# The opening of a two-block kernel: norm sums on GpSimd, one load queue, matmuls on zeros, and a gate unit in two passes

## The reference

```python
def rmsnorm(x, g):
    xf = x.astype(jnp.float32)
    y = xf * lax.rsqrt(jnp.mean(xf * xf, axis=-1, keepdims=True) + EPS)
    return (y * g.astype(jnp.float32)).astype(x.dtype)

h = rmsnorm(x, ln_g[l])
proj = h @ w_in[l]            # split into g_u, g_v, ..., d_a, d_b, c_q, c_z
g = -jnp.exp(dn_a_log) * jax.nn.softplus(d_a + dn_dt_bias)
beta = jax.nn.sigmoid(d_b)
m = rmsnorm(mem, mem_norm_g[l])
mk, mv = jnp.split(m @ w_mem_kv[l], 2, axis=-1)
```

## Time and profile before

| | us |
|---|---|
| median of 3 runs | 2020.8 (2020.19 to 2021.98) |
| the profiled execution | 2021.16 |
| its span | 2019.6 |
| PE busy | 1981.8 (98%) |
| DVE busy | 1135.0 (56%) |
| ACT busy | 838.9 (42%) |
| POOL busy | 144.1 (7%) |

### The profile page before, as it was taken

One profiled execution on the slowest core, in us unless ns is written; L12 is line 12 of the kernel. 1 busy time (PEld: TensorE's weight loads), 2 busy tenths in 40 slices (PEclk: granted clock), 3 DMA queues, 4 the chain that ended last, 5 costly groups with the idle time before them and its releaser, 6 DMA issues.

```text
span 2019.6 us, 28731 instructions
## 1 busy us (share of the span) xinstructions
PE 1981.8 (98%) x9560; PEld 1647.7 (82%) x9560; DVE 1135.0 (56%) x1982; ACT 838.9 (42%) x1627; POOL 144.1 (7%) x174
## 2 busy tenths in 40 slices
PE   7999999999999999999999999999999999998999
PEld 6788788888888888788878888888888888887887
DVE  5643576777767775643355454545454545455332
ACT  5543444444444443533245353535353535354211
POOL 1100011121111210011000000000000000000110
PEclk9999999999999999999999999999999999998999
DMA  9522231222322212244422222222222222222441
GB/s 364 197 95 83 73 94 64 72 73 73 75 76 77 73 63 76 81 159 149 150 99 84 89 83 88 83 88 83 88 83 88 83 88 83 88 83 86 153 151 68
DMA packets 33394, 202.32 MB, mean 100 GB/s; under 512 B 4528, under 2 KB 4656, under 8 KB 12624
## 3 DMA queue, kind: packets, MB, share of 16 engines
q1 hardware_dynamic: 23040, 164.64, 22.8%
q0 software_dynamic: 10176, 37.13, 6.4%
q10 hardware_dynamic: 144, 0.10, 0.0%
HBM read 193.43 MB, written 8.42 MB: 100 GB/s over the span
## 4 chain that ended last, share of the span: by engine, by line
PE 93%; ACT 2%; DVE 2%; DMA 1%; issue 1%; POOL 0%; DVEq 0%; ACTq 0%; SPq 0%; POOLq 0%
PE gemm L1222 80%; PE pb L1222 12%; PE pb L1225 2%; DMA scratch<-in_memT 1%; ACT scratch L613 0%; DMA raw<-in_w 0%; ACT w_hi_t L617 0%; ACT scratch L615 0%; ACT scratch L368 0%; DVE scratch L1094 0%; DMA scratch<-in_rows_in 0%; DVE w_lo_t L1138 0%; DVE w_lo L663 0%; ACT w_hi L327 0%; DVE scratch L1133 0%
## 5 line engine op out<-in xcount | busy, mean ns | idle before, releaser
L1222 PE MATMUL gemm<-act_lo,w_hi 128*128 128x512 f32 x2512 | 979.2, 392 | 12.2 <-DVE act_lo L684 10.2
L1222 PE MATMUL gemm<-act_hi,w_hi 128*128 128x512 f32 x2384 | 956.7, 401 | 13.2 <-DVE act_lo L672 10.5
L1222 PE MATMUL gemm<-act_hi,w_lo 128*128 128x512 f32 x2384 | 932.5, 391 | 0.0
L1222 PEld LDWEIGHTS gemm<-act_lo,w_hi 128*128 128x128 f32 x2512 | 475.9, 189 | 106.3 <-issue 14.5
L1222 PEld LDWEIGHTS gemm<-act_hi,w_hi 128*128 128x128 f32 x2384 | 449.7, 189 | 105.3 <-issue 19.3
L1222 PEld LDWEIGHTS gemm<-act_hi,w_lo 128*128 128x128 f32 x2384 | 448.5, 188 | 96.3
L327 ACT ACTIVATE w_hi<-raw 128x512 fp32r<-128x512 f32 x624 | 341.0, 618 | 407.7 <-PE gemm L1222 394.8
L663 DVE TENSOR_TENSOR w_lo<-raw,w_hi 128x512 fp32r<-128x512 f32 x624 | 402.6, 701 | 189.8 <-ACT w_hi L327 188.0
L1222 PEld LDWEIGHTS pb<-scratch 128*128 128x128 f32 (+1 forms) x1248 | 163.3, 188 | 29.2 <-DVE scratch L989 4.9
L1222 PE MATMUL pb<-scratch 128*128 128x64 f32 (+4 forms) x1248 | 173.4, 277 | 1.5 <-DVE scratch L989 1.2
L265 POOL TENSOR_TENSOR scratch<-scratch,cst 128x512 f32<-128x512 f32 x56 | 78.4, 1405 | 433.7 <-DVE scratch L882 262.4
(11 more groups left out here) (226 smaller groups left out, 1453.8 us busy)
## 6 DMA issues: line engine op xcount, KB each, us to landing
raw<-in_w SPq DMA_DIRECT2D x156, 1024.0 KB, 4.8
scratch<-in_rows_in POOLq DMA_DIRECT2D x6, 1024.0 KB, 6.1
big<-in_xT POOLq DMA_DIRECT2D x4, 1024.0 KB, 11.8
scratch<-rows POOLq DMA_DIRECT2D x16, 256.0 KB, 6.0
scratch<-in_xT POOLq DMA_DIRECT2D x16, 256.0 KB, 3.0
x<-big POOLq DMA_DIRECT2D x16, 256.0 KB, 2.3
scratch<-x POOLq DMA_DIRECT2D x16, 256.0 KB, 4.0
outT<-scratch POOLq DMA_DIRECT2D x16, 256.0 KB, 3.8
```

Source lines behind the costliest of these rows:

```text
L1222: return nc.tensor.matmul(out, a, b, start=start, stop=stop, skip_group_check=skip)
```

## The change

It does five things.

- The norm sums no longer come from row-major copies. ACT squares the feature-major tiles (memT in place, xT into free tiles), POOL adds the squares up with nine additions (`fold` and three additions of 128 x 2048), and PE multiplies the remaining tile with ones. ACT takes the root on the spread result. `rows_in`, the diagonals and their loads are gone.
- memT and xT are loaded by SP's queue, between the weights: w quarter, memT quarter, four times; then the quarters of w 1; then w 2, xT 0, w 3, xT 1 and so on. POOL loads only the constants, after unit 1 has been multiplied.
- PE begins with six fp32 matmuls on a tile of zeros.
- The gate unit holds high and low part of its 64 used columns side by side in one stationary operand, and needs two matmuls a k step, not three; the two halves are added after the transposes.
- The sums over ones come after step 3 of unit 9; the gate transposes come before the ones of the memory values, and both factors of the memory projection are applied before these transposes.

Shortened to what matters:

```diff
-MT, XT = 2, 4
-ROW_AT = {3: 0, 5: 1}
+MT = 2
+X_SQ = {1: 0, 2: 1, 3: 2, 4: 3}
...
+        MVF, MR = tl(20, 2), tl(22)[:, 0:MEM]
+        XSQ = [tl(0, 4), tl(12, 4), tl(8, 4), tl(12, 4)]
+        WARM = tl(1)
...
@@ SP @@
             for q in range(4):
+                c, m = slice(q * S, (q + 1) * S), slice(4 * q * MEM, 4 * (q + 1) * MEM)
+                sp.dma_start(raw[0][:, c], w[0][:, c]).then_inc(sem[f"early_in{q}"], 16)
+                sp.dma_start(MEMRAW[:, m], memT[:, m]).then_inc(sem[f"tile_in{q}"], 16)
+            for q in range(4):
                 c = slice(q * S, (q + 1) * S)
-                sp.dma_start(raw[0][:, c], w[0][:, c]).then_inc(sem[f"early_in{q}"], 16)
-            load(1, 1)
-            with sp.Fori(0, (U_END - 3) // 2) as i:
+                sp.wait_ge(sem["hi"], q + 1)
+                sp.dma_start(raw[1][:, c], w[1][:, c]).then_inc(sem[f"early_in{q}"], 16)
+            for q in range(4):
+                sp.wait_ge(sem["hi"], 4 * q + 4)
+                sp.wait_ge(sem["lo"], 4 * q + 4)
+                load(q + 2, q % 2)
+                sp.dma_start(blk(big[:, :], NB * NB * q, NB * NB).rearrange("p (k t) -> p k t", t=S),
+                             xT[4 * q:4 * q + 4].rearrange("k p t -> p k t")).then_inc(sem[f"tile_in{q}"], 16)
+            with sp.Fori(2, (U_END - 3) // 2) as i:
...
@@ POOL @@
+            st = Steps(pool, sem["x_sum"])
+
+            def fold(t, n):
+
+                st.then(nc.gpsimd.tensor_tensor(t[:, 0:n], t[:, 0:n], t[:, n:2 * n], ALU.add))
+
+            pool.wait_ge(sem["unit"], 2)
             pool.dma_start(cst[:, :], consts).then_inc(sem["cst_in"], 16)
...
+            pool.wait_ge(sem["x_sq"], 2)
+            for n in range(4):
+                fold(MEMRAW, KT * MEM >> n + 1)
+            for q in range(1, 4):
+                pool.wait_ge(sem["x_sq"], 2 + q + 1)
+                st.then(nc.gpsimd.tensor_tensor(XSQ[0], XSQ[0], XSQ[q], ALU.add))
+            fold(XSQ[0], 2 * S)
+            fold(XSQ[0], S)
...
@@ ACT @@
+            def packed_hi():
+
+                act.wait_ge(sem["w_in0"], 8 * U_AB)
+                act.wait_ge(sem["unit"], U_AB - 1)
+                for q in range(4):
+                    c = slice(q * S, (q + 1) * S)
+                    A(v3(w_hi[0][:, c])[:, :, 0:H], v3(raw[0][:, c])[:, :, 0:H], ACT.Copy).then_inc(sem["hi"], 1)
...
+            def x_squares(q):
+                act.wait_ge(sem[f"tile_in{q}"], 32)
+                if q >= 2:
+
+                    act.wait_ge(sem["x_sum"], {2: 1, 3: 5}[q])
+                A(XSQ[q], blk(big[:, :], NB * NB * q, NB * NB), ACT.Square).then_inc(sem["x_sq"], 1)
...
-                if u in ROW_AT:
-                    row_squares(ROW_AT[u])
+                if u == 0:
+
+                    act.wait_ge(sem["act_lo"], KT)
+                    for j in range(2):
+                        m = slice(j * NB * S, (j + 1) * NB * S)
+                        A(MEMRAW[:, m], MEMRAW[:, m], ACT.Square).then_inc(sem["x_sq"], 1)
+                if u in X_SQ:
+                    x_squares(X_SQ[u])
             hi(U_AB + 1, (U_AB + 1) % 2)
-            for t in range(MT, MT + XT):
-                row_squares(t)
...
+            act.wait_ge(sem["x_ps"], 1)
+            st.then(A(XR, pb[1][:, :], ACT.Ln, bias=eps[:, 0:1], scale=1.0 / D))
+            A(XR, XR, ACT.Exp, scale=-0.5).then_inc(sem["x_r"], 1)
+            act.wait_ge(sem["x_ps"], 2)
+            st.then(A(MR, pb[5][:, 0:MEM], ACT.Ln, bias=eps[:, 0:1], scale=1.0 / D))
+            A(MR, MR, ACT.Exp, scale=-0.5).then_inc(sem["x_r"], 1)
             hi(U_V + 1, (U_V + 1) % 2)
...
@@ DVE @@
+            V.memset(WARM, 0.0).then_inc(sem["init"], 1)
...
-                if u < 7:
+                if u < 6:
                     lo(u + 2, u % 2)
+                elif u == 6:
+
+                    for q in range(4):
+                        dve.wait_ge(sem["hi"], 4 * U_AB + (q + 1))
+                        c = slice(q * S, (q + 1) * S)
+                        wh = v3(w_hi[0][:, c])
+                        V.tensor_tensor(wh[:, :, H:P], v3(raw[0][:, c])[:, :, 0:H], wh[:, :, 0:H].bitcast(F32), ALU.subtract).then_inc(sem["lo"], 1)
...
+            for t in (MK, MVF):
+                heads = t.rearrange("p (h m) -> p h m", m=MEM)
+                V.tensor_tensor(heads, heads, MR.rearrange("p (h m) -> p h m", h=1).broadcast_to([P, XA, MEM]), ALU.mult)\
+                    .then_inc(sem["mv_tok"], 1)
...
@@ PE @@
+            pe.wait_ge(sem["init"], 2)
+            for _ in range(6):
+                mm(pb[0][:, 0:MEM], WARM[:, 0:P], WARM[:, 0:MEM])
             for u in range(8):
                 mem_gemm(u)
 
-            gemm(U_AB, U_AB % 2, before=KT)
-            gemm(U_V, U_V % 2, 0, 5)
-            pe.wait_ge(sem["diag"], 1)
-            mm(pb[1][:, :], C["ones"], DIAG[:, MT * P:(MT + XT) * P]).then_inc(sem["x_ps"], 1)
-            mm(pb[5][:, 0:MEM], C["ones"], DIAG[:, 0:MT * P]).then_inc(sem["mr_ps"], 1)
-
-            pe.wait_ge(sem["evac"], 8)
+            pe.wait_ge(sem["evac"], U_AB - 1)
+            for k in range(KT):
+                if k % 4 == 0:
+                    pe.wait_ge(sem["hi"], 4 * U_AB + (k // 4 + 1))
+                    pe.wait_ge(sem["lo"], 4 * U_AB + (k // 4 + 1))
+                pe.wait_ge(sem["act_hi"], KT + k + 1)
+                pe.wait_ge(sem["act_lo"], KT + k + 1)
+                both = w_hi[0][:, k * P:(k + 1) * P]
+                mm(bank[0][:, :], both, act_hi[:, k * S:(k + 1) * S], k == 0, False)
+                ins = mm(bank[0][:, :], both, act_lo[:, k * S:(k + 1) * S], False, k == KT - 1)
+            ins.then_inc(sem["unit"], 1)
+            gemm(U_V, U_V % 2, 0, 3)
+            pe.wait_ge(sem["cst_in"], 16)
+            pe.wait_ge(sem["x_sum"], 9)
+            mm(pb[1][:, :], C["ones"], XSQ[0][:, 0:S]).then_inc(sem["x_ps"], 1)
+            mm(pb[5][:, 0:MEM], C["ones"], MEMRAW[:, 0:MEM]).then_inc(sem["x_ps"], 1)
+            gemm(U_V, U_V % 2, 3, 13)
+            pe.wait_ge(sem["evac"], U_AB + 1)
...
+            pe.wait_ge(sem["mv_tok"], 2)
             for b in range(MT):
                 for n in range(XA):
                     ins = tp(pb[2 + b][:, n * P:(n + 1) * P], MVF[:, n * MEM + b * P:n * MEM + (b + 1) * P])
                 ins.then_inc(sem["mv_ps"], 1)
-            gemm(U_V, U_V % 2, 5, 13)
```

More of the change, by code:

```diff
@@ L83, in leave, with build @@
         self.base, self.n = self.start + times * self.per, 0
-def build(nc, w, xT, memT, rows_in, consts, negatives, params, ws_t, bs_b, rel, x1_dram, rows_dram, outT):
+def build(nc, w, xT, memT, consts, negatives, params, ws_t, bs_b, rel, x1_dram, rows_dram, outT):
     with ExitStack() as ctx:
@@ L155, in build @@
         MEMRAW, XR = tl(4, 8), tl(15)
[L156 to L160, removed]
+        MVF, MR = tl(20, 2), tl(22)[:, 0:MEM]
+        XSQ = [tl(0, 4), tl(12, 4), tl(8, 4), tl(12, 4)]
+        WARM = tl(1)
+        wsT, bsb, SUMS_IN = tl(26), tl(27), tl(24)[:, 0:2 * P]
         def blk(a, c, n=1):
@@ L184, in build @@
         names = """consts_in cst_in par_in tile_in0 tile_in1 tile_in2 tile_in3 early_in0 early_in1 early_in2 early_in3 w_in0 w_in1 hi lo unit evac act_hi act_lo
-            mem_free row_sq diag mr_ps x_ps x_r
+            mem_free x_sq x_sum x_ps x_r
             mv_tok mv_ps mixed
@@ L319, in hi @@
             def hi(u, slot):
[L322 removed]
+                act.wait_ge(sem[f"w_in{slot}"], 8 * u - 8 * slot)
                 if not isinstance(u, int) or u >= 2:
@@ L354, in _, with early_hi @@
             act.wait_ge(sem["init"], 1)
-            act.wait_ge(sem["par_in"], 16)
+            def early_hi(slot, q):
+                c = slice(q * S, (q + 1) * S)
+                act.wait_ge(sem[f"early_in{q}"], 16 * slot + 16)
+                A(w_hi[slot][:, c], raw[slot][:, c], ACT.Copy).then_inc(sem["hi"], 1)
             for q in range(4):
-                c = slice(q * S, (q + 1) * S)
-                act.wait_ge(sem[f"early_in{q}"], 16)
-                A(w_hi[0][:, c], raw[0][:, c], ACT.Copy).then_inc(sem["hi"], 1)
+                early_hi(0, q)
+                if q == 0:
+                    act.wait_ge(sem["par_in"], 16)
                 act.wait_ge(sem[f"tile_in{q}"], 16)
@@ L363, in _ @@
                       scale=par[:, C_MEM + k:C_MEM + k + 1]).then_inc(sem["act_hi"], 1)
[L364 to L368, removed]
+            for q in range(4):
+                early_hi(1, q)
+            def x_squares(q):
[3 more added lines that the diff above has]
+                A(XSQ[q], blk(big[:, :], NB * NB * q, NB * NB), ACT.Square).then_inc(sem["x_sq"], 1)
             for u in range(7):
-                hi(u + 2, u % 2)
+                if u + 2 == U_AB:
+                    packed_hi()
+                else:
+                    hi(u + 2, u % 2)
                 for k in X_HI.get(u, ()):
@@ L726, in _ @@
             bias8 = par[:, C_DT:C_DT + DN].rearrange("p (c h) -> p c h", c=1).broadcast_to([P, NB, DN])
```

(16 more changed lines are left out.)

37 lines of the change are left out of this document (7 added, 30 removed).

## The result

The changed kernel takes 2027.51 us (median of 8, 2026.03 to 2029.46); the kernel before took 2020.24 in the same series (8, 2019.73 to 2021.98). The ratio is 1.0035, with a 95% interval of 1.0024 to 1.0046: slower by 7.3 us, where 2.9 were forecast. The profiled execution of after took 2029.46 (span 2027.9).

A forecast was written before the change was run, and what follows sets the result against it. PE, busy 98%, was taken as the bound. POOL's start at 24.3, 52.5 of lock and 1.5 of rest gave 78.3; with 18.0 the sums end at 96.3, 2.5 us later than before: 2023.7 us, range 2011.5 to 2029.5.

The forecast's parts named there:

- The likeliest case: Opening: POOL additions and DVE two-input instructions exclude each other, binding as summed; 2.5 us later, 2023.7; chance 0.50.
- POOL's start: Opening: POOL begins adding when both mem squares are done, after unit 2's load at 18.5; forecast 24.3 us.
- POOL's own time: POOL's nine additions, 11520 columns, priced at 0.10 us fixed each plus a rate per column: 27.8 us.
- DVE's share of the lock: DVE's w_lo of units 3 to 7 (12.3), the packed ones (1.7) and the act_lo (10.7).
- The lock's rest: Time from POOL's start to the last act_lo in which the lock carries nothing: taken as 1.5 us.
- the load of unit 4: Opening: w4 lands at 31, late by xT in the queue, for a unit 4 start at 32.5: hidden.
- case 4: Opening: POOL wins the lock twice running, late w_lo delay loads, the clock falls; 2028 to 2031; chance 0.15.
- cases 1 and 4: Case 1: the lock binds as summed, 2023.7, chance 0.50. Case 4: worse, with missed loads, 2028 to 2031, chance 0.15.
- The tail: From the last act_lo to the end of the gates' cumulative sums, through U_V, sums and transposes: 18.0 us.
- The case without a conflict: Opening: POOL's additions hold up no DVE instruction; sums at 83.2 against 93.80, 10.6 us gained, 2010.6; chance 0.15.

The follow-up runs named there:

- e1: The changed kernel with POOL's nine additions cut to two columns each, leaving out most of the norm sums: 2016.35 us.
- e7: The changed kernel with two-column POOL additions and the gate unit in three passes as before: 2017.63 us.
- e6: The changed kernel with two-column POOL additions and without the six matmuls on zeros: 2014.60 us.
- e11: The changed kernel with PE summing ACT's fp32r squares instead of POOL's additions, xT one load later, no matmuls on zeros: 2012.98 us.
- e5x: The changed kernel with two-column POOL additions, constants issued after unit 4 and each xT tile one load later: 2014.16 us.
- e5: The changed kernel with two-column POOL additions and POOL issuing the constants after unit 4 instead of after unit 1: 2014.57 us.
- e8: The changed kernel with whole POOL additions, xT one load later, constants behind POOL's first x addition and unit 4: 2028.43 us.
- e3: The kernel before with one POOL memset and five 128x2048 POOL additions from unit 2 on, which nothing reads: 2033.87 us.
- e4: The kernel before with only the new load order and the matmuls on zeros, row tiles on POOL's queue behind the constants: 2023.91 us.

## Why the prediction was right, and where too small

The likeliest case had the mechanism and the sign: DVE's two-input instructions and POOL's additions shut each other out, the summed time sets the end of x_low, and the rest follows. The range held the time, but it was 18 us wide and the time lies near its upper end, and "slower" had a chance of 0.27 against 0.45 for "same": that the range held says little, the experiments on the lock say more. The size of the effect was short: the sums were forecast at 96.3 and came at 101.1, so 4.8 us are missing. By the prediction's own terms:

- **POOL's start, forecast 24.3, was 27.08: +2.8.** memT 0 landed at 7.52, not 6.1, so the first matmul came at 8.78; and unit 2's load landed at 21.17, not 18.5. I had taken 4.6 us for it, less than the 5.5 of the earlier trace rows, but it was 6.16, with xT 0 right behind it in the queue. These are rates of transfer that I took too well.
- **POOL's own time, forecast 27.8, was about 26.3: -1.5.** The 2048-column additions took 4.54 and 4.59 where 4.9 was taken. This row of after, min/median/max in ns, has all three of x, one of which waited:

```profile
L258 POOL TENSOR_TENSOR scratch<-scratch x3: 4545/4588/5005, 42.8 to 54.4; 128x2048 f32<-128x2048 f32 x3
```

  The Trainium skill's figure of 4497 ns (GPSIMD Engine Reference, Elementwise — side-by-side cycle accounting) was nearer than my scaling of the earlier trace rows; the runs agree with it to 2%. My error was the fixed part: an addition of 2 columns takes 197 ns (e1), and I had taken the memset's 0.10. With 0.20 fixed and 2.125 ns a column, from the 4545 above, the nine additions are an estimated 26.3 us. Their busy time in the trace was 28.4; six of them waited about a third to half a microsecond for a w_lo.
- **DVE's share of the lock, forecast 24.7, was about right.** (12.3 + 1.7 + 10.7; the four packed ones took 1.43 together, not 1.7, and the rest came at its pace where nothing held it.)
- **The lock's rest, forecast 1.5, was 4.5: +3.0. This is the term that was mis-sized most; the step behind it that failed is the load of unit 4, taken as hidden.** From 27.08 to the last x_low at 82.57 are 55.5 us, less 26.3 and 24.7. The trace shows where neither engine held the lock, 6.2 us in all (the held pieces overlap a little at the hand-overs, so this is more than 4.5). From 40.81 to 42.77 POOL waited for a square that ACT made behind the late high part of unit 4, and DVE, after a reduction, for unit 5. "w4 is late by this first, at 31, for a start of unit 4 at 32.5: hidden" was wrong: it was issued at 24.43 and landed at 36.76, and the chain goes through it. The constants, 1.4 MB that I let "share the engines with w3", lay beside it. From 67.57 to 69.93 there was nothing to carry but unit 8's load, issued only behind the late w_lo of 6 at 64.79 and landed at 69.46. The other 1.8 us are four stretches in which DVE made a reduction of a unit (0.60 each); the sum of the lock had no term for these at all. A late w_lo delays the load of the unit after next, which is what case 4 said; the time lay between the points of cases 1 and 4.
- **The tail, forecast 18.0, was 18.55: +0.5.**

Together +2.8 - 1.5 + 3.0 + 0.5 = 4.8. The 2.8 and the 3.0 come for the greater part from loads taken as faster than they were, and the price of POOL's additions hid a part of it.

Steps that held: a single w_lo reached 5.08 us; PE waited 3.5 us at unit 3; the gate unit ran at DVE's pace (e7); POOL ended its sums at 63.4 and PE reached them at 85.5, so nobody waited for the sums themselves; the zeros cost and bring nothing (e6, e11). The case without a conflict, forecast at 83.2 for the sums and 2010.6, is e5x with 86.5 and 2014.2. Of the 3.3 us, 1.4 are the later start (unit 1 at 17.3, not 15.9), 1.0 the wait at 46.80 that e5x makes itself, and 0.5 the tail.

Where it could have been better is the weighing of the load of unit 4. The chain of before shows a weight load of 8.32 us, and two that it doesn't show, issued at 28.70 and 32.56 beside xT, constants and row tiles, took 9.2 and 10.3 us. A queue with 1 MB of xT behind each 1 MB of weights and 1.4 MB of constants beside them was no place to count on 6.5.

The end of x_low did not follow from the sum alone, since PE's clock fell three times, at each of the windows shown; I charged nothing for that, as DVE set the pace there. The chain of after supports this (DVE and its loads, not PE, from 15 to 77), but no run separates the clock from the waits. Of the span's 8.3 us, 1.0 is lost behind the sums. Behind 105 us the trace of after has 21.9 us at the lower clock and that of before 20.6, which is up to 0.6 of it; the rest is open, and the medians differ by 7.3 only.

## What to carry to other kernels

Before work is moved to an idle engine, look at what the two engines share and not at their busy shares: POOL was idle for 92% of the span and its 26 us still cost 11. Add up the busy time of the instructions that exclude each other, with what the engine must do besides, and compare it with the stretch. Where it was more than the stretch had, cutting into pieces won back 3 of 11 us here, while another engine, with the loads of e5x, won back 10 to 14, most of all the one that had gaps because it waited for the bottleneck. An edit that moves one step of an engine's fixed program moves all behind it: e5, e5x and e8 each made a wait of their own that way. And when weights must arrive on time, every megabyte queued between or beside them belongs into the sum.

## What the runs showed that I had not expected

- Chained additions on POOL let DVE through once between two of them: four w_lo beside four additions took 10.26 us, one each in turn. Before, one w_lo had stood through two POOL multiplies, so this turn-taking isn't always there; what makes the difference no run shows. A w_lo that waited ends some 0.55 us after the POOL instruction does, against 0.68 for one alone.
- Not every DVE instruction is shut out: in e8 a reduction, whose one input is in PSUM, began at 58.27 inside an addition (57.87 to 62.77) and took its usual 0.68 us.
- The fixed part of a POOL addition is about 0.2 us, by e1:

```profile
L258 POOL TENSOR_TENSOR scratch<-scratch x3: 197/197/197, 42.2 to 53.1; 128x2 f32<-128x2 f32 x3
```

  The rest is 2.1 ns a column. With the same tile as both inputs (e3) five additions took 19.6 us, waits for w_lo included: under 4 us each, cheaper than the 4.55 of two different inputs.
- A weight load of 1 MB landed in 4.67 us with nothing behind it (after, at 64.79), in 6.16 with another load behind it, in 12.3 with an xT tile before it and constants beside, and in 17.0 with constants and row tiles beside (e4, unit 5). The same order of loads gave 9.9 instead of 12.3 in e6.
